# Seven products for eight in a short convolution's projections, beside a stream of cache pages

## What is computed

```python
def conv_mixer(a, state, w_in, w_conv, w_out):
    gb, gc, v = jnp.split(a @ w_in, 3, axis=-1)
    u = gc * v
    u_ext = jnp.concatenate([state.astype(u.dtype), u], axis=1)
    t = a.shape[1]
    conv = w_conv[0] * u_ext[:, 0:t]
    for k in range(1, CONV_WIDTH):
        conv = conv + w_conv[k] * u_ext[:, k:k + t]
    return (gb * conv) @ w_out, u_ext[:, t:]
```

## Time and profile before

| what | value |
|---|---|
| median of 3 timed runs | 1291.38 us (1289.93 to 1296.14) |
| profiled execution, first to last instruction (span) | 1291.9 us |
| TensorE busy (products, weight loads) | 1210.7 us (94%), 1006.9 us (78%) |
| VectorE, ScalarE, GpSimd busy | 467.1 us (36%), 282.3 us (22%), 197.9 us (15%) |
| DMA | 326.44 MB, mean 253 GB/s |
| mean granted TensorE clock | 0.982 |

### The profile page before, as it was taken

The page is one execution under the profiler, slowest core; times in us unless marked ns, Lnnn a source line. Parts: engine busy times, 40 slices in busy tenths (PEclk is TensorE's granted clock), DMA queues, the critical chain, the costliest instruction groups (busy, mean ns, idle before and its releaser), DMA issues.

```text
span 1291.9 us, 38852 instructions
## 1 busy us (share of the span) xinstructions
PE 1210.7 (94%) x16250; PEld 1006.9 (78%) x16250; DVE 467.1 (36%) x1372; ACT 282.3 (22%) x757; POOL 197.9 (15%) x335
## 2 busy tenths in 40 slices
PE   7999999999999998997787879989999999999998
PEld 5887786999999976574345457787898888978876
DVE  2110115677774331004676763421221211212213
ACT  1000003101010021235876861210010000100122
POOL 3012122012340000233345440000000000000000
PEclk9999999999999998999898989999999999999999
DMA  9786879998344264464477776498988879889831
GB/s 311 292 324 238 303 264 314 181 371 311 113 150 175 104 260 177 143 126 137 145 254 217 228 251 252 175 409 330 388 308 346 334 302 394 312 317 367 321 128 37
DMA packets 108352, 326.44 MB, mean 253 GB/s; under 512 B 15512, under 2 KB 33769, under 8 KB 106516
## 3 DMA queue, kind: packets, MB, share of 16 engines
q1 hardware_dynamic: 90868, 263.71, 55.2%
q0 software_dynamic: 16160, 59.96, 15.4%
q10 hardware_dynamic: 1152, 0.30, 0.1%
HBM read 316.65 MB, written 14.52 MB: 256 GB/s over the span
## 4 chain that ended last, share of the span: by engine, by line
PE 87%; DVE 5%; issue 3%; ACT 2%; DMA 1%; POOLq 0%; POOL 0%; ACTq 0%; DVEq 0%
PE bank L1944 20%; PE bank L2543 15%; PE bank L2046 12%; PE pbank L2554 6%; PE bank L2082 6%; PE bank L2000 5%; PE pbank L2543 3%; PE bank L2554 3%; PE bank L2525 3%; PE bank L2150 2%; PE bank L2512 1%; PE bank L2177 1%; PE bank L2317 1%; PE bank L2272 1%; PE pbank L2512 1%
## 5 line engine op out<-in xcount | busy, mean ns | idle before, releaser
L2543 PE MATMUL bank<-X,gring 128*64 128x96 f32 x4608 | 196.0, 247 | 6.1 <-issue 6.1
L2543 PEld LDWEIGHTS bank<-X,gring 128*64 128x64 f32 x4608 | 191.9, 137 | 10.6 <-issue 10.6
L1944 PE MATMUL bank<-aT,gring 128*128 128x288 f32 x768 | 192.7, 410 | 3.5 <-DVE aT L1286 3.5
L1944 PEld LDWEIGHTS bank<-aT,gring 128*128 128x128 f32 x768 | 146.6, 192 | 46.0 <-issue 5.8
L2554 PE MATMUL pbank<-Q,X 128*32 128x256 f32 x1152 | 76.0, 379 | 0.0
L2046 PE MATMUL bank<-aT,gring 128*128 128x144 f32 x528 | 72.1, 286 | 0.0
L1865 DVE TENSOR_TENSOR hT<-hT,bank 128x288 f32<-128x288 f32 x48 | 18.9, 448 | 146.4 <-PE bank L2512 146.4
L2000 PE MATMUL bank<-Q,X 128*64 128x64 f32 x2048 | 63.3, 223 | 7.9 <-issue 7.9
L2000 PEld LDWEIGHTS bank<-Q,X 128*64 128x64 f32 x2048 | 61.3, 138 | 11.9 <-issue 11.5
L1872 DVE TENSOR_TENSOR X<-X,bank 128x96 f32<-128x96 f32 x72 | 18.4, 256 | 141.5 <-ACT X L1232 140.9
L2046 PEld LDWEIGHTS bank<-aT,gring 128*128 128x128 f32 x528 | 67.7, 190 | 0.0
(11 more groups left out here) (380 smaller groups left out, 1814.7 us busy)
## 6 DMA issues: line engine op xcount, KB each, us to landing
gring<-in_moe SPq DMA_DIRECT2D x176, 512.0 KB, 5.7
Q<-in_moe SPq DMA_DIRECT2D x72, 512.0 KB, 7.0
gring<-in_dense_gu SPq DMA_DIRECT2D x44, 512.0 KB, 13.4
Q<-in_cache_cmp POOLq DMA_DIRECT2D x64, 256.0 KB, 5.7
Q<-in_cache_cmp SPq DMA_DIRECT2D x64, 256.0 KB, 5.6
gring<-in_conv_in SPq DMA_DIRECT2D x24, 512.0 KB, 10.2
gring<-in_dense_down SPq DMA_DIRECT2D x16, 704.0 KB, 5.4
gring<-in_ple_gate SPq DMA_DIRECT2D x16, 512.0 KB, 5.6
```

Of the source, the lines that this page charges most:

```text
L1944: ins = pe.matmul(bank(label, k)[:, 0:T], tile[:, 128 * i:128 * i + 128], rhs[:, i, :], start=i == 0, stop=i == C - 1)
L2543: ins = pe.matmul(m_bank(i, M_GU + f)[64 * w:64 * w + 64, CAP * u:CAP * u + CAP], gslot(("m", 0), 2 * f + u)[:, o:o + 64], ae[:, c, :], st ...
```

## The change

The 24 input tiles and 8 output tiles of the convolution become 16 pairs that use the form of the dense stage; CI = 12 input pairs, CO = 4 output pairs, DN = 16. The dense pairs follow in the same numbering, 16 to 37. For channel chunks 2m and 2m + 1 the input pairs are (gc, v) of 2m, (gc, v) of 2m + 1, (gb of 2m, gb of 2m + 1). Weight sums and token differences are formed by VectorE; `norm`, `add_to_h` and the convolution's taps are rearranged around them. The batches of compression stand behind other tiles than before.

```diff
+CI, CO = 12, 4
+DN = CI + CO
+WN = DN + HALVES * FC
+COMPRESS_AFTER = {4: 0, 5: 1, 7: 2, 8: 3, 10: 4, 11: 5, 12: 6, 13: 7}
...
+            def pair_loads(first, last):
+                for k in range(first, last):
+                    n = k // 2
+                    if n < CI:
+                        c = 2 * (n // 3) + (n % 3 == 1)
+                        src = A["conv_in"][3 * c + k % 2] if n % 3 < 2 else A["conv_in"][3 * (c + k % 2) + 2]
+                    elif n < DN:
+                        src = A["conv_out"][k - 2 * CI]
+                    else:
+                        src = A["dense_gu"][(k - 2 * DN) // (2 * FC), (k - 2 * DN) % (2 * FC)]
+                    g_load(("w", k), src)
...
-            for c in range(3):
-                conv_loads(c)
+            pair_loads(0, 10)
             sp.wait_ge(ptab_in, 16)
             early_pages(0)
             late_pages(0)
             for k in range(4):
                 sp.dma_start(wc[:, 32 * k:32 * k + 32, :], A["w_cmp"][:, 32 * k:32 * k + 32, :]).then_inc(wcmp_in, 16)
-            conv_loads(3)
+            pair_loads(10, 12)
             early_pages(1)
+            pair_loads(12, 15)
             for b in range(1, B):
                 late_pages(b)
                 if b + 1 < B:
                     early_pages(b + 1)
...
+                pair_loads(12 + 3 * b, min(15 + 3 * b, 2 * DN))
+            pair_loads(2 * DN, 2 * WN)
...
 ScalarE
+            for n in range(DN):
+                first_product(n)
+                if n > CI:
+                    for c in range(2 * (n - CI) - 2, 2 * (n - CI)):
+                        norm_square(1, c)
+                if n in COMPRESS_AFTER:
+                    compressed(COMPRESS_AFTER[n])
+                if n == CI + 1:
+                    for b in range(B):
+                        drained(act, ("ck", b))
+                    for a in range(2):
+                        act.activation(kcsq[:, a, :], kcn[:, a, :], ACT.Square).then_inc(kcsq_ready, 1)
             for a in range(2):
                 rstd(kcscale[a], bank(("css", a))[:, :], ("css", a))
+            for c in range(C - 2, C):
+                norm_square(1, c)
...
 VectorE
+            def token_sum(s, k, x, sums):
+
+                low, high = x[:, 0:4, :], x[:, 4:8, :]
+                t1, t2, t4 = sums
+                if k == 0:
+                    ins = dve.tensor_tensor(t1, low[:, :, HT:T], low[:, :, 0:HT], ALU.subtract)
+                elif k == 1:
+                    dve.wait_ge(t_sums_ready, 4 * s + 1)
+                    ins = dve.tensor_tensor(low[:, :, HT:T], high[:, :, HT:T], low[:, :, HT:T], ALU.subtract)
+                elif k == 2:
+                    ins = dve.tensor_tensor(t2, high[:, :, HT:T], t1, ALU.subtract)
+                else:
+                    dve.wait_ge(t_sums_ready, 4 * s + 3)
+                    ins = dve.tensor_tensor(t4, high[:, :, 0:HT], t2, ALU.subtract)
+                ins.then_inc(t_sums_ready, 1)
...
+            def pair_sums(n, following):
+
+                a, part, u = bank(("ha", n)), part_of(n), conv_u2 if n < DN else u2
+                full(dve, ("ha", n))
+                dve.wait_ge(p1_copied, n + 1)
+                chain(dve.tensor_tensor(u, part[:, 0:HT], a[:, 2 * HT:3 * HT], ALU.add))
+                if following:
+                    weight_sum(n + 2, 0)
+                settled()
+                chain(dve.tensor_tensor(two(part[:, HT:3 * HT]), both_halves(u), two(a[:, 0:2 * HT]), ALU.add))
+                if following:
+                    weight_sum(n + 2, 1)
+                settled()
...
+            for k in range(4):
+                weight_sum(0, k)
+            scaled_by(("norm", 0))
+            for c in range(4):
+                normalized(0, c)
+            dve.wait_ge(a_ready, 4)
+            token_sum(0, 0, aT, conv_t_sums)
+            for c in range(4, 8):
+                normalized(0, c)
+            dve.wait_ge(a_ready, 8)
+            for k in range(1, 4):
+                token_sum(0, k, aT, conv_t_sums)
+            for k in range(4):
+                weight_sum(1, k)
...
+            for n in range(CI):
+                c = 2 * (n // 3) + n % 3
+                pair_out(n, sg[:, 0, :], sg[:, 1, :], True)
+                settled()
+                drained(dve, ("hb", n))
+                if n % 3 < 2:
+                    gated(c)
+                else:
+                    for i in range(2):
+                        dve.tensor_tensor(zT[:, c - 2 + i, :], sg[:, i, :], tmp[:, i, :], ALU.mult).then_inc(z_ready, 1)
+            full(dve, ("hb", CI - 1))
+            dve.wait_ge(z_ready, C)
+            for k in range(4):
+                token_sum(1, k, zT, conv_t_sums)
...
+            def pair_added(n):
+
+                a, b, part = bank(("ha", n)), bank(("hb", n)), part_of(n)
+                gate, up = hT[:, 2 * (n - CI), :], hT[:, 2 * (n - CI) + 1, :]
+                pair_sums(n, True)
+                chain(dve.tensor_tensor(two(up), two(up), both_halves(part[:, 2 * HT:3 * HT]), ALU.add))
+                chain(dve.tensor_tensor(gate, gate, part[:, 0:2 * HT], ALU.add))
+                settled()
+                drain(dve.tensor_tensor(up[:, HT:T], up[:, HT:T], a[:, 0:HT], ALU.add), ("ha", n))
+                full(dve, ("hb", n))
+                chain(dve.tensor_tensor(up[:, 0:HT], up[:, 0:HT], b[:, 2 * HT:3 * HT], ALU.add))
+                settled()
+                drained(dve, ("ha", n))
+                drain(dve.tensor_tensor(gate, gate, b[:, 0:2 * HT], ALU.add), ("hb", n))
+                weight_sum(n + 2, 2)
+                weight_sum(n + 2, 3)
+
+            for n in range(CI, DN):
+                pair_added(n)
+                if n == DN - 2:
+                    compressed_keys()
+                    for c in range(1, 4):
+                        add_squares(1, c)
+            for c in range(4, C - 1):
+                add_squares(1, c)
+            norm(1)
...
 TensorE
-            for c in range(C):
-                for name in ("gc", "v", "gb"):
-                    g_linear((name, c), aT, ready=0 if c == 0 and name == "gc" else None)
-                if c >= 2:
-                    compress(c - 2)
...
+            for n in range(DN):
+                if n == 0:
+                    pe.wait_ge(a_ready, 4)
+                elif n == CI:
+                    pe.wait_ge(z_ready, 4)
+                elif n == DN - 1:
                     pe.wait_ge(ident_in, 16 * NIDENT)
                     for a in range(2):
                         bank_free(pe, ("css", a))
                         pe.wait_ge(kcsq_ready, a + 1)
                         fill(pe.matmul(bank(("css", a))[:, :], bones[:, :], kcsq[:, a, :], start=True, stop=True), ("css", a))
...
+                pair_product(n, aT if n < CI else zT, n // CI, conv_t_sums)
+                if n in COMPRESS_AFTER:
+                    compress(COMPRESS_AFTER[n])
```

More of the change, by code:

```diff
@@ L176, in g_tile_order @@
     o = []
-    for c in range(C):
-        o += [("gc", c), ("v", c), ("gb", c)]
-    o += [("co", c) for c in range(C)]
-    o += [("f", k) for k in range(2 * FT)]
+    o += [("w", k) for k in range(2 * WN)]
     o += [("skip",)] + [("d", i) for i in range(2 * GS)]
@@ L287, in trunk @@
         tiles += [tS[:, 0:GT], tS[:, GT:2 * GT], Q[:, 8832:8832 + GT]]
-        kcscale = [tS[:, 1024 + 512 * a:1536 + 512 * a] for a in range(2)]
-        kcsq = tS[:, 0:1024].rearrange("p (a n) -> p a n", a=2)
         ohs = [Q[:, HALF:HALF + KEYS], Q[:, HALF + KEYS:HALF + KEYS + 672]]
@@ L509, in gslot, with sums_of, part_of @@
             return gring[:, s * GT:(s + 1) * GT]
+        def sums_of(n):
+            return conv_sums[n % 2] if n < DN else half_sums[n % 2]
+        def part_of(n):
+            return conv_parts[n % 2] if n < DN else parts[n % 2]
         def by_pool(label):
@@ L1411, in dense_hidden @@
+                up = tmp[:, 1, :]
+                pair_out(DN + n, tmp[:, 0, :], up, n + 2 < FT)
                 s = sg[:, n % 2, :]
@@ L2106, in dense @@
                 pe.wait_ge(a_ready, ready)
-                for n in range(FT):
-                    dense_hidden(n)
+                for n in range(DN, WN):
+                    pair_product(n, aT, 2, t_sums)
                 for j in range(C // 2):
```

340 lines of the change are left out of this document (140 added, 200 removed).

## The result

The changed kernel takes 1316.57 us (median of 4 runs, 1310.42 to 1324.02), the kernel before, run beside it, 1292.84 us: a ratio of 1.0186, 95% interval 1.0144 to 1.0229, about 24 us slower. I had forecast 14 us slower, 1305.5 us, within 1293 to 1315: that it is slower is right, the size is not. The profiled execution is the slowest of the four (1324.02 us), 7 us above the median. Its span is 30.4 us longer than that of before: 25.8 us of that lie in the first 403 us, and 4.6 us in the rest, which the change doesn't touch (there all traces of this case, 18 with those of the experiments, last between 907.2 and 919.4 us, and this one is the longest). I use it for the first 403 us; terms of one to three us read off it are within what executions of one program can differ by.

A forecast was written before the change was run, and what follows sets the result against it. TensorE was taken to bound the page-streaming stage, with pages only 0.2 to 1.7 us early. Sum: -0.8 (to batch 7) + 10.9 (tail) + 5 (clock) - 1 (issue waits) = +14 us, 1305.5 us, range 1293 to 1315.

The forecast's parts named there:

- What bounds the stage: Up to the dense stage: TensorE bounds; late pages land 10.2 to 11.6 us after a batch, 0.2 to 1.7 us early.
- The middle: Gaps between batches: one-pair gaps wait for pages, 18.8 us of new waiting; batch 7 ends at 203.6 us against 204.4.
- Pair 12's second product: Before batch 6: TensorE waits 2.4 us for VectorE, held at a late weight tile; hidden in the page wait.
- The start: Up to batch 0: norm ready at 15.05 us, pair 0 ends at 25.0, batch 0 at 60.1 against 58.5.
- The tail: From batch 7 to the dense stage: 29.4 us for 18.5, so 10.9 us longer, 5.2 us of it TensorE idle.
- The clock: Behind the six new waits TensorE falls to half speed, 1.65 us each: 0 to 9.9 us, half taken, 5 us.
- issue waits: TensorE's waits inside batches may shrink where it idled before: 0 to 7 us less for five batches, 1 us taken.
- Nothing behind 222.9 us is changed, so it hands the delay on: Dense stage and after: runs without a TensorE gap, one pair in 6.87 us, and keeps its length.
- rival 3: Clock falls at all six new waits and VectorE adds a 2 us wait: +22 us, 1313 us; chance 0.13.

The follow-up runs named there:

- experiment 10: Changed kernel with the input half undone, pairs 0 to 11 made as two 288-column tiles each in the same places: 1314.2 us, 1.0178.
- Experiment 1: Kernel before with its old 288-column tiles, only the eight compression batches moved to where the change puts them: 1318.1 us, 1.0206.
- experiment 5: Kernel before, with cache pages loaded only for batch 0 and one half of batch 1: 1282.98 us, 0.9935.
- 6: Changed kernel, with cache pages loaded only for batch 0 and one half of batch 1: 1285.3 us, 0.9964.
- experiment 14: Kernel of experiment 12, with ScalarE's queue issuing two of the eight pages of each late half: 1287.25 us, 0.9968 to the kernel before.
- 15: Changed kernel, with ScalarE's queue issuing two of the eight pages of each late half: 1306.27 us, 1.0123.
- 16: Kernel before, with ScalarE's queue issuing two of the eight pages of each late half, as control: 1288.97 us, 0.9986.
- 3: Changed kernel, with VectorE's compressed keys and two weight sums of pair 17 moved behind the last square sums: 1307.79 us, 1.0112.
- 2: Changed kernel with 28 to 48 filler products put where TensorE waits, which proved too long: 1325.6 us, 1.0269.
- experiment 7: Changed kernel with 14 to 22 filler products put where TensorE waits, a little under the waits they fill: 1309.71 us, 1.0165.
- 9: Changed kernel with the output half undone, pairs 12 to 15 made as two 288-column tiles each, batches in place: 1305.95 us, 1.0107.
- 4: Changed kernel with batches one and a half pairs apart, at the places of the kernel before, and VectorE's end order of experiment 3: 1298.11 us, 1.0050.
- 8: Kernel of experiment 4, with SyncE issuing a period's three weight tiles ahead of its early pages: 1300.05 us, 1.0071 to the kernel before.
- 11: Changed kernel with pair 0 alone made as two tiles, its weight sums left out: 1306.0 us, 1.0122.
- experiment 12: Changed kernel with pair 0 and output pairs 12 to 15 as tiles, batches at the places of the kernel before: 1291.05 us, 0.9998.
- 13: Kernel of experiment 12, with pages loaded only for batch 0 and one half of batch 1: 1277.63 us, 0.9888 to the kernel before.

## Why the forecast had the right sign and the wrong size

- **What bounds the stage: right, and it decides.** With two queues issuing, the last page lands 9.6 to 12.5 us after the batch before in 83 of 84 cases (13.4 us once, in experiment 10), whatever TensorE does meanwhile. Experiment 1 shows it without any new product, 10 without the input pairs, 5 and 6 without the pages, 14 to 16 by shortening the loop.
- **The middle: right in mechanism, short in size.** Forecast gaps 10.2, 10.6, 10.2, 10.5, 11.6; measured 10.5, 10.8, 10.6, 11.7, 12.0. With the two-pair gaps that is 2.8 us more. Pair 12's second product waited 1.1 us (2.4 forecast).
- **The start: 2.7 us late in this execution, in good part by chance.** Tile 1, forecast "some 2.7 us behind, at 12.4", landed at 14.2, and the norm behind the weight sums started at 17.14 for 15.05. But in the kernel before it landed at 12.3, and in the 16 experiments at 11.7 to 13.2; only the profiled execution of the change has it later. Batch 0 of the changed kernel's start ended at 60.9 and 61.7 us in experiments 3 and 15, for 60.1 forecast and 62.8 here. The clock fell at the start in all of them (16.5 to 19.4 us), which the forecast did not count.
- **The tail: right to 0.3 us step by step.** From batch 7's end, forecast and measured: pair 15 starts 8.7, 8.8; ScalarE's passes end 13.6, 13.3; keys 14.4, 14.1; squares 15.9, 15.6; norm product 22.5, 22.3. What followed was not: "6.9 us behind it as before" was 10.2. Experiments 2, 7 and 9, in which the clock stays up there, have 6.7 to 6.8 us, and those in which it falls 10.1 to 10.8 (3, with a shorter fall, 8.4): this price is shown.
- **The clock: the step that failed most.** It was taken at 5 us, "I take half", less 1 for issue waits. Clock falls came at five of the six new waits (not at batch 6) and at the start, not at half of them, and lasted 3.4 to 10.2 us, not 3.3; two of the eight falls that the forecast had counted in the trace of before had lasted 6.8 and 10.2 us already. Against the forecast's terms the batches are 3.1 us longer, the tail 3.3, and the fall in the dense stage costs 1.7: 8 us. Of these the tail's is shown; the batches' is not parted from what the issue waits gave back. Experiment 7's 7 us do not confirm the sum, though the number is near: its batches got no shorter in all, and 1.5 of the 8.3 us that its trace gained by 403 us stand at batch 0 and 1.5 in a shorter issue wait of the dense stage.

  The rule of the Trainium skill, "TensorE: Matmul & The Clock Gate" (HAM oscillation), that each burst after a DMA wait starts cold, fits these traces better than my halving did: over all traces without filler products, a fall stands at 18 of the 21 waits of over 3 us ahead of a batch, and at 8 of the 23 of 1.3 to 3 us. Half of the 28 busy us at half speed would be 14 us: a batch at half speed waits less for its instructions (batch 3: 10.17 us, at half speed for its first 5.6 us, and no issue wait; 9.3 us before with one), so part of the loss is covered.
- **"Nothing behind 222.9 us is changed, so it hands the delay on": wrong by 4.1 us.** The dense stage got an issue wait of 2.26 us at 259.24, and the clock fell behind it (1.7 us more). It appeared in the changed kernel and in experiments 3, 6 and 15, with 2.0 to 2.5 us; it was 0.7 us in experiment 7, and the first part lasts 145.8 us, as before, in 2, 4 and 8 to 14. Experiments 1 and 5, which have no new pairs, show it too (1.65 and 0.95 us), so it is not the pairs' own. Why it falls where it does is open.

The sum by these measured sizes: 14 + 2.7 + 2.8 + (8.1 - 4) + 2.3 = 25.9 us in the profiled execution, against 25.8 read off and 24 by the medians. It adds up the rows of the table again, so it checks the reading and not the causes. No rival was right alone; rival 3 (22 us) came nearest, with its clock, not with its VectorE wait.

What the prediction did not ask is why the pairs, placed well, earn nothing. Experiments 12 to 14 give part of the answer. In experiment 12 the pairs between batch 0 and batch 7 make the gaps cheaper by 7.2 us (75.2 us in experiment 14, where nothing waits for pages, for 82.4 before), and 2.5 us of that arrive: the other 4.7 us are the page loop, which was already nearly as long as three tiles and a batch. The batches then take 2.7 us more, with issue waits of 10.8 us for 7.9 and one fall of the clock inside a batch. Whether issue waits grow because the same traffic is packed more densely is not shown: experiment 14 packs it more densely still, and its issue waits are 8.6 us. No run changed the issue waits alone.

## What to carry to other kernels

Before making an engine's work cheaper, find the loop that runs beside it and its length; where the margin is 0.2 to 1.7 us, a saving of 1.5 us a period (three tiles in 10.3 us for 11.8) brought 0.4 us a period in the gaps (experiment 12), until the loop was shortened too. Move work in a stream of transfers only with its period kept: the new places of the batches made 19 us of page waits here, more than the products saved (16 us). Read a term of two us off several executions, not off one. Price both ends of a stage apart, and do not assume that the stage behind runs as before: its instructions and its clock arrive with the history of the stage ahead.

## What the runs showed of the hardware

- **TensorE's instructions are fetched during the run, and later beside a stream of pages.** One queue of the trace moves packets of 16 KB named "instruction", 20 between 50 and 215 us. The DMA view of the change, 259 to 260 us:

```profile
q8 instruction: 1, 0.02, 5.5%
```

  It starts at 259.09 and takes 0.88 us; TensorE's issue wait ends at 261.50, 1.53 us after its end. The same holds everywhere: of 93 issue waits of over 0.4 us between 25 and 300 us in all 18 traces, those ahead of a batch left out, every one ends 1.2 to 1.6 us after such a packet has ended. The 1.3 us of "issue" in the earlier trace rows is one of them. With pages in the air the packets of this stage are hardly slower (their median is 1.0 to 1.1 us in every kernel; the longest took 1.98 us, in experiment 10, and 1.44 in the three kernels without pages), but they start later: in the kernel before, the seven packets ahead of its seven waits start 30 to 96 product instructions further on in the program than the same packets in experiment 5, the same program without pages. What holds their start back is not shown.
- A stretch at half speed made batches 1, 3, 5 and 7 of the change 2.3, 0.9, 0.5 and 0.6 us longer than the same batches of before (8.4, 9.3, 9.4 and 9.3 us), though it halves TensorE's clock for 3.4 or 6.8 us. Three of the four had a shorter issue wait than before or none; that the slower batch does not outrun its instructions is my reading.
- SyncE issues a 256 KB page in about 1.0 us, GpSimd in 1.15; a third queue, ScalarE's, took two of eight and brought the late half in early enough to end the page waits in experiment 14.
